# GpSimd prepares 48 weight chunks of the last mixer early and keeps their bf16 halves in DRAM; the last mixer's side work runs at four steps a chunk

## The chip, the cores and the metric

The kernel runs on one core of a Trainium2 chip. The metric is the device time in microseconds (us), the median of several runs. PE is TensorE, DVE is VectorE, ACT is ScalarE, POOL is GpSimd, SP is SyncE. L12 is line 12 of the kernel before.

## The reference

One sequence of 256 tokens, width 2048, goes through two blocks of two layers each. Cut to what matters:

```
first block (2 layers):
    short-conv mixer:  y = b * conv3(c * xv), then @ w_out
    conv FFN:          h = conv3(x @ w_up) + b;  (silu(g) * u) @ w_down
    shared k, v and differential attention;  conv FFN again
second block:
    ab_layer: dilated attention + gated linear attention, gate, @ w_out
    cd_layer (the last mixer):
        u, qd, fd, idd, gate = split(h @ cd_w_in)
        yc = s5_mixer(u)                 # complex diagonal state, scanned over time
        f  = lb + (1 - lb) * sigmoid(fd)
        od = chunked_gated_linear_attention(silu(qd), 1 - f, idd, log f)   # 8 heads ("hgrn")
        y  = concat(yc * sigmoid(yc @ w_glu + b), norm(od)) * silu(gate)
        h  = h + y @ cd_w_out
    final rmsnorm
```

All weights come as float32 and the products have to be near float32.

## The kernel before, in words

Activations lie transposed, features on partitions, 256 tokens along the free axis. Every large product is cut into weight chunks of 512 rows by 512 columns (1 MB of float32), 535 of them, in the fixed order of `weight_groups`. A group of chunks (four in most cases, two where an operand has 1024 rows) shares one PSUM tile; two PSUM tiles (PSG) alternate. A chunk goes through four engines:

- SP loads it into the ring WF of 3 slots (`load`, L410, the DMA at L415). It may do so once DVE is through with the chunk 3 before.
- ACT rounds it to bf16 into WH, a ring of 5 (`hi`, L994, the copy at L999), and adds one to `s_hi`. It waits for the load and for the matmuls of the chunk 5 before.
- DVE writes WL = WF - WH in bf16, again a ring of 5 (`lo`, L1485, the subtraction at L1489), and adds one to `s_lo`.
- PE waits for `s_lo` and issues 48 matmuls (`gemm`, L538, the matmul at L531): each 128x128 piece meets x as high x high, high x low, low x high. Then it adds one to `s_mm`.

ACT and DVE run `LA = 3` chunks ahead of PE, by the order in which their programs are written.

Everything that isn't a large product (attention, scans, norms) is a **side flow**, a Python generator on each engine. `side.step()` issues the next piece of the flow, and `gemm(..., rate=r)` decides how many pieces go beside one chunk: PE takes one after the second of the chunk's four row blocks and `max(1, r - 1)` behind the chunk; ACT and DVE take r. `side.until(flow)` issues all that is left of a flow at once. Every engine's order is fixed when the program is written.

In the last mixer the groups come in the order u (8 chunks), fd, qd, idd (8 each), three gate groups (12), glu (4), the last gate group (4), cd_out0 (8) and cd_out1 (8). Behind u two side flows start. `s5` has 16 iterations; in each PE multiplies the inputs (`product`), DVE does 10 instructions (L2070 to L2091, the scan at L2081 among them), and PE reads the result out into PSUM; after each second iteration DVE adds that (L2097). POOL's queue loads a rotation table for each iteration and output weights for each second one, ACT fills the scan's decay. `hgrn` has 8 heads: POOL subtracts the decays (`decays`, L438, lines 449 to 452), ACT exponentiates (L1291), DVE weights them (L1904), PE makes two sets of 8 products, DVE masks and sums each (L1914, L1918), PE multiplies with v and takes the norm. With rate 3, `hgrn` ends in front of cd_out1.

POOL is idle from 1.2 us on until the second FFN of the first block at 1487 us. The scratch SCR has a free stretch at `TR` until the attention of the first block (the stages before it are the first mixer, its output, and the first FFN: 196 chunks).

```
nc.vector.wait_ge(s_hi, i + 1)
tt(l, w, h, ALU.subtract).then_inc(s_lo, 1)          # lo(i), DVE
nc.tensor.wait_ge(s_lo, i + 1)                       # gemm, PE
if kk == 1 and rate > 1:
    side.step()
last.then_inc(s_mm, 1)
for _ in range(max(1, rate - 1)):
    side.step()
```

Of the kernel before, what the change touches and what calls it, by code (L numbers as in the profile page):

```python
# [195 lines left out]
def two_block_model(nc, A, out):  # L196
    ctx = ExitStack()
    with ctx:
# [10 lines left out]
        WH = sb("WH", [128, RB, 4, 512], BF16)  # L209
        WL = sb("WL", [128, RB, 4, 512], BF16)  # L210
# [17 lines left out]
        d_w = [sem(f"d_w{i}") for i in range(RF)]  # L228
        d_out = [sem(f"d_out{i}") for i in range(2)]
# [37 lines left out]
        groups, stage, chunks = weight_groups(A)  # L267

# [92 lines left out]
        T1, T2, T3 = (scr(TR + 3840 + 512 * n, 2, T) for n in range(3))  # L361
        CSD = nc.dram_tensor("s5_rotation", (16, 128, 4 * T), F32).ap()
# [46 lines left out]
        def sync_program():  # L409
            def load(i):  # L410
                g, k0, rows = chunks[i]
                src = g["w"][k0:k0 + rows, g["col"]:g["col"] + g["width"]].rearrange("(t p) n -> p t n", p=128)
                if i >= RF:
                    nc.sync.wait_ge(s_lo, i - RF + 1)
                nc.sync.dma_start(shaped(WF, i % RF, rows, g["width"]), src).then_inc(d_w[i % RF], 16)  # L415
# [9 lines left out]
            for i in range(RF, len(chunks)):  # L425
# [9 lines left out]
        def gpsimd_program():  # L435
# [21 lines left out]
            nc.gpsimd.memset(CX[:, :, 0:2], 0.0).then_inc(s_ones, 1)  # L457

# [67 lines left out]
        def tensor_program():  # L526
# [11 lines left out]
            def gemm(gi, xh, xl, ready=None, row_major=False, rate=1, before=None, tail=None):  # L538
# [6 lines left out]
                for c, k0 in enumerate(g["rows"]):  # L545
# [5 lines left out]
                    nc.tensor.wait_ge(s_lo, i + 1)  # L551
# [411 lines left out]
            for name in ("fd", "qd"):  # L963
                for gi in stage[name]:
                    gemm(gi, xh, xl, rate=3)
            for gi in stage["idd"]:
                gemm(gi, xh, xl, row_major=True, rate=3)
            flags.add("idd")
            for gi in stage["cd_gate"][0:3]:
                gemm(gi, xh, xl, rate=3)  # L970
            side.until(s5_flow)
            uh, ul = columns_of(UH), columns_of(UL)
            for n, gi in enumerate(stage["glu"]):
                gemm(gi, uh, ul, [(s_ul, k // 4 + 1) for k in range(8)] if n == 0 else None, rate=3)
            gated_0 = side.add_first(gated((0,)))
            gemm(stage["cd_gate"][3], xh, xl, rate=3)
            gated_1 = side.add_first(gated((1,)))
            gated_h = side.add(gated((2, 3)))
            residual("cd_out0", None, uh, ul, [(s_gl, 5 + k // 4) for k in range(8)], rate=3,
# [8 lines left out]
        def scalar_program():  # L988
# [446 lines left out]
            for j, gi in enumerate(stage["fd"]):  # L1435
                keep(gi, four(FF, j), 3, func=ACT.Sigmoid)
                nc.scalar.wait_ge(s_kd, j + 1)
                act(four(FF, j), four(FF, j), ACT.Ln).then_inc(s_fg, 1)
            for j, gi in enumerate(stage["qd"]):
                keep(gi, four(QH, j), 3, func=ACT.Silu)  # L1440
            for j, gi in enumerate(stage["idd"]):
                keep(gi, VI[:, :, 512 * j:512 * j + 512], 3, row_major=True)
# [21 lines left out]
            keep(gates[3], four(GT1, 1), 3, func=ACT.Silu)  # L1464
# [7 lines left out]
            residual("cd_out0", None, rate=3, before=lambda c: side.until(gated_0, *((gated_1,) if c else ())))  # L1472
# [6 lines left out]
        def vector_program():  # L1479
# [658 lines left out]
            for j, gi in enumerate(stage["fd"]):  # L2138
                gemm(gi, rate=3)
# [11 lines left out]
            for gi in stage["qd"] + stage["idd"]:  # L2151
                gemm(gi, rate=3)
            flags.add("idd")
            gates = stage["cd_gate"]
            for gi in gates[0:3]:
                gemm(gi, rate=3)
            side.until(s5_flow)
            for j, gi in enumerate(stage["glu"]):
                gemm(gi, rate=3)
# [14 lines left out]
            gemm(gates[3], rate=3)  # L2174
# [9 lines left out]
            residual("cd_out0", None, rate=3, before=lambda c: side.until(gated_0, *((gated_1,) if c else ())))  # L2184
# [70 lines left out]
```

## Time and profile before

| | |
|---|---|
| median of 3 runs | 3213.49 us (3213.07 to 3217.09) |
| the profiled execution: its own time | 3213.27 us |
| the profiled execution: span of the trace | 3212.0 us |
| PE busy | 3055.3 us, 95% |
| PE weight loads busy | 2600.1 us, 81% |
| DVE busy | 2129.2 us, 66% |
| ACT busy | 1527.7 us, 48% |
| POOL busy | 164.7 us, 5% |
| HBM read, written | 577.32 MB, 15.73 MB |

The matmuls are pipelined, so PE's busy time is not PE at its peak. A share of busy time is an average over stages with different limits; what the change touches are two stretches, the first 1084 us and the last 520 us, and they are to be read apart.

### The profile page before, as it was taken

What the parts mean: (1) busy time and instruction counts of PE and PEld (TensorE: products, weight loads), DVE (VectorE), ACT (ScalarE), POOL (GpSimd) and SP (SyncE); (2) the same over time, 40 slices, a digit from 0 to 9 for tenths busy, and PEclk for the clock granted to TensorE, in tenths of its full rate; (3) what the DMA queues carried; (4) which work ended last, traced back from release to release, by engine and by line L of the source; (5) the groups of instructions that cost most, each with busy time, mean ns of one, the idle gap of its engine ahead of it and who ended that gap; (6) DMA issues with size and microseconds to landing.
All of it is one profiled execution on the core that took longest, in us unless ns stands there. A gap on an engine that the chain in (4) does not pass through costs nothing. (4 is left out here: it accounts for less than half of the span.)

```text
span 3212.0 us, 57240 instructions
## 1 busy us (share of the span) xinstructions
PE 3055.3 (95%) x25845; PEld 2600.1 (81%) x25870; DVE 2129.2 (66%) x2024; ACT 1527.7 (48%) x1406; POOL 164.7 (5%) x292
## 2 busy tenths in 40 slices
PE   8999899999999999999999999998999899789896
PEld 7888788888888787587888888887686787657785
DVE  5555766666556666458687786555665547898785
ACT  4343654445434544745555555334554534333652
POOL 0000000000000000001200000000400000002220
PEclk9999999999999999999999999999999999899998
DMA  8665456655656454445766666563545445554331
GB/s 287 208 205 191 139 203 210 209 197 195 225 185 210 149 172 167 169 158 166 260 236 213 228 230 216 205 202 115 171 157 188 167 171 186 171 184 168 119 135 62
DMA packets 295477, 596.75 MB, mean 186 GB/s; under 512 B 11825, under 2 KB 16049, under 8 KB 295105
## 3 DMA queue, kind: packets, MB, share of 16 engines
q1 hardware_dynamic: 287616, 564.22, 51.4%
q0 software_dynamic: 7616, 28.87, 2.4%
q8 instruction: 203, 3.33, 0.4%
q14 instruction: 42, 0.34, 0.0%
HBM read 577.32 MB, written 15.73 MB: 185 GB/s over the span
## 5 line engine op out<-in xcount | busy, mean ns | idle before, releaser
L1489 DVE TENSOR_TENSOR WL<-WF,WH 128x2048 bf16<-128x2048 f32 x533 | 1208.5, 2288 | 682.3 <-ACT WH L999 682.1
L531 PE MATMUL PSG<-XH,WH 128*128 128x256 bf16 x5648 | 1549.9, 274 | 52.4 <-DVE XL L1594 26.3
L531 PE MATMUL PSG<-XL,WH 128*128 128x256 bf16 x5648 | 1549.7, 274 | 0.0
L531 PE MATMUL PSG<-XH,WL 128*128 128x256 bf16 x5648 | 1548.8, 274 | 0.0
L999 ACT ACTIVATE WH<-WF 128x2048 bf16<-128x2048 f32 x533 | 999.9, 1899 | 615.4 <-PE PSG L531 372.2
L531 PE MATMUL PSG<-SCR,WH 128*128 128x256 bf16 x4480 | 736.8, 273 | 0.0
L531 PEld LDWEIGHTS PSG<-XH,WH 128*128 128x128 bf16 x5648 | 556.4, 99 | 134.7 <-issue 65.5
L531 PEld LDWEIGHTS PSG<-XL,WH 128*128 128x128 bf16 x5648 | 555.9, 98 | 69.9 <-issue 1.2
L531 PEld LDWEIGHTS PSG<-XH,WL 128*128 128x128 bf16 x5648 | 556.1, 98 | 67.8
L531 PE MATMUL PSG<-SCR,WL 128*128 128x256 bf16 x2240 | 610.6, 273 | 0.0
L531 PEld LDWEIGHTS PSG<-SCR,WH 128*128 128x128 bf16 x4480 | 438.5, 98 | 55.0
L531 PEld LDWEIGHTS PSG<-SCR,WL 128*128 128x128 bf16 x2240 | 219.2, 98 | 25.5
L531 PE MATMUL PB<-SCR 128*128 128x128 f32 (+3 forms) x928 | 165.9, 347 | 53.0 <-DVE SCR L2091 32.2
L531 PEld LDWEIGHTS PB<-SCR 128*128 128x128 f32 (+2 forms) x928 | 137.1, 206 | 75.8 <-DVE SCR L2091 36.9
L1713 DVE SCALAR_TENSOR_TENSOR SCR<-PSG,PR,SCR 128x254 f32<-128x254 f32 (+1 forms) x352 | 143.9, 474 | 54.9 <-ACT SCR L1172 53.8
L1172 ACT ACTIVATE SCR<-PSG,PR 128x256 f32<-128x256 f32 x176 | 84.9, 562 | 102.6 <-PE PSG L531 102.4
L1020 ACT ACTIVATE SCR<-PSG 128x1024 f32<-128x1024 f32 x34 | 34.7, 1021 | 181.8 <-PE PSG L531 181.8
L531 PE MATMUL PSG<-WL,XH 128*128 128x512 bf16 x314 | 119.3, 380 | 1.0 <-issue 0.5
L531 PE MATMUL PSG<-WH,XL 128*128 128x512 bf16 x314 | 119.3, 380 | 0.3
L531 PE MATMUL PSG<-WH,XH 128*128 128x512 bf16 x307 | 116.8, 381 | 0.3
L461 POOL DMA_DIRECT2D SCR<-s_cT_re x1 | 0.7, 696 | 1486.2 <-DVE XL L1594 1486.2
L1183 ACT ACTIVATE SCR<-SCR 128x1024 bf16<-128x1024 f32 x22 | 23.2, 1057 | 96.1 <-DVE SCR L1722 96.1
(240 smaller groups left out, 1652.5 us busy)
## 6 DMA issues: line engine op xcount, KB each, us to landing
WF<-ffn_w_up SPq DMA_DIRECT2D x176, 1024.0 KB, 5.8
WF<-ffn_w_down SPq DMA_DIRECT2D x88, 1024.0 KB, 5.1
WF<-ab_w_in SPq DMA_DIRECT2D x56, 1024.0 KB, 5.2
WF<-a_w_in SPq DMA_DIRECT2D x48, 1024.0 KB, 6.0
WF<-cd_w_in SPq DMA_DIRECT2D x48, 1024.0 KB, 5.2
WF<-a_w_out SPq DMA_DIRECT2D x16, 1024.0 KB, 5.1
WF<-kv_w_k SPq DMA_DIRECT2D x16, 1024.0 KB, 5.1
WF<-b_w_q SPq DMA_DIRECT2D x16, 1024.0 KB, 5.1
```

Of the source, the lines that this page charges most:

```text
L461: nc.gpsimd.dma_start(CT[i].rearrange("p a b -> p (a b)"), A[name]).then_inc(d_s5c, 16)
L531: return nc.tensor.matmul(o, lhsT, rhs, start=start, stop=stop, skip_group_check=True)
L999: act(shaped(WH, i % RB, rows, g["width"]), shaped(WF, i % RF, rows, g["width"]), ACT.Copy).then_inc(s_hi, 1)
L1020: act(dst, rowwise(ps) if row_major else ps[:, :, :], func, scale=scale).then_inc(s_evac[gi % 2], 1)
L1172: t = act(dst[:, n, :], ps[:, n, :], ACT.Identity, bias=pr("f_bias", 88 * l + f), scale=pr("f_conv", 264 * l + 176 + f))
L1183: act(four(HH, j), HF, ACT.Copy).then_inc(s_hh, 1)
L1489: tt(l, w, h, ALU.subtract).then_inc(s_lo, 1)
L1713: ins = stt(dst[:, n, sh:T], ps[:, n, 0:T - sh], pr("f_conv", 264 * l + 88 * tap + f), dst[:, n, sh:T], ALU.mult, ALU.add)
```

## The change

The last mixer's first 48 chunks behind u (fd, qd, idd, all gates, glu and half of cd_out0) become **kept** chunks. From the sixth finished WL on, POOL takes them in 96 pieces of 256 rows: it loads a piece into scratch (512 KB), casts it to bf16, stores the high half (256 KB), subtracts, and stores the low half (256 KB), all into a DRAM tensor `weight_halves`. In the last mixer SP loads both halves of a kept chunk with one DMA of 1 MB straight into the ring of bf16 halves; ACT's cast and DVE's subtraction of these chunks are gone, and PE waits for the DMA. SP in front of the first kept load, and ACT in front of the first attention group, wait until all 96 pieces are stored. WH and WL become two views of one tensor WS. From fd on to cd_out0, rate 3 becomes rate 4.

```diff
-        WH = sb("WH", [128, RB, 4, 512], BF16)
-        WL = sb("WL", [128, RB, 4, 512], BF16)
+        WS = sb("WS", [128, RB, 2, 4, 512], BF16)
+        WH, WL = WS[:, :, 0, :, :], WS[:, :, 1, :, :]
...
+        first_kept = groups[stage["fd"][0]]["first"]
+        HALVES = nc.dram_tensor("weight_halves", (KEPT, 128, 2, 2048), BF16).ap()
...
+        KW = scr(TR, 2, 512)
+        KH, KL = scr(TR + 1024, 2, 512, dt=BF16), scr(TR + 1536, 2, 512, dt=BF16)
...
             def load(i):
+                if kept(i):
+                    nc.sync.wait_ge(s_mm, i - RB + 1)
+                    nc.sync.dma_start(WS[:, i % RB], HALVES[i - first_kept].rearrange("p h (t n) -> p h t n", n=512)
+                                      ).then_inc(d_ws[i % RB], 16)
+                    return
...
+            nc.sync.wait_ge(d_kh, 32 * KEPT)
+            nc.sync.wait_ge(d_kl, 32 * KEPT)
+            for i in range(first_kept, len(chunks)):
                 load(i)
...
+            def keep(n):
+
+                g, k0, rows = chunks[first_kept + n // 2]
+                a = 1024 * (n % 2)
+                src = g["w"][k0 + a // 4:k0 + a // 4 + 256, g["col"]:g["col"] + 512]
+                nc.gpsimd.dma_start(KW, src.rearrange("(t p) n -> p t n", p=128)).then_inc(d_keep, 16)
+                to_h, to_l = (HALVES[n // 2][:, i, a:a + 1024].rearrange("p (t n) -> p t n", n=512) for i in range(2))
+                nc.gpsimd.wait_ge(d_keep, 16 * (n + 1))
+                if n:
+                    nc.gpsimd.wait_ge(d_kh, 16 * n)
+                t = own.mark(nc.gpsimd.tensor_copy(KH, KW))
+                nc.gpsimd.wait_ge(g_own, t)
+                nc.gpsimd.dma_start(to_h, KH).then_inc(d_kh, 16)
+                if n:
+                    nc.gpsimd.wait_ge(d_kl, 16 * n)
+                t = own.mark(nc.gpsimd.tensor_tensor(KL, KW, KH, ALU.subtract))
+                nc.gpsimd.wait_ge(g_own, t)
+                nc.gpsimd.dma_start(to_l, KL).then_inc(d_kl, 16)
+
+            nc.gpsimd.wait_ge(s_lo, 6)
+            for n in range(2 * KEPT):
+                keep(n)
...
-                    nc.tensor.wait_ge(s_lo, i + 1)
+                    nc.tensor.wait_ge(*halves_there(i))
...
             def hi(i):
+                if kept(i):
+                    return
...
             pairs, outs = [], []
+            nc.scalar.wait_ge(d_kh, 32 * KEPT)
+            nc.scalar.wait_ge(d_kl, 32 * KEPT)
...
             def lo(i):
+                if kept(i):
+                    return
...
-                gemm(gi, rate=3)
+                gemm(gi, rate=4)
```

What it moves, at three places. The names are those of the program; SCR is the scratch, PB the PSUM banks of the side flows, PSG those of the large products.

POOL, start of the program. Before, a table load of the second FFN follows the memsets:

```order
L457 MEMSET SCR 128x4x2
L461 DMA SCR<-s_cT_re 128x512
L461 DMA SCR<-s_cT_im 128x512
L462 MEMSET SCR 128x1280
```

Now:

```order
L488 MEMSET SCR 128x4x2
L495 DMA SCR<-cd_w_in 128x2x512
L500 CAST SCR<-SCR 128x1024
L502 DMA weight_halves<-SCR 128x1024
L505 ISA
L505 TENSOR_TENSOR SCR<-SCR 128x1024
L507 DMA weight_halves<-SCR 128x1024
```

Five of these rows (without ISA) come 96 times in front of everything that POOL did before.

DVE, last mixer, one iteration of s5 in the middle of the gate groups, before:

```order
L2070 TENSOR_TENSOR SCR<-PB,SCR 128x1024
L2071 TENSOR_TENSOR SCR<-PB,SCR 128x1024
L2073 TENSOR_TENSOR SCR<-SCR 128x512
L2074 TENSOR_TENSOR SCR<-SCR 128x512
L1489 TENSOR_TENSOR WL<-WF,WH 128x2048
L2081 SCALAR_TENSOR_TENSOR SCR<-SCR 128x512 x2
L2086 TENSOR_TENSOR SCR<-SCR 128x1024
L2088 TENSOR_TENSOR SCR<-SCR 128x1024
L2090 TENSOR_TENSOR SCR<-SCR 128x512
L2091 TENSOR_TENSOR SCR<-SCR 128x512
L1489 TENSOR_TENSOR WL<-WF,WH 128x2048
L2097 SCALAR_TENSOR_TENSOR SCR<-SCR,PR,PB 128x256
```

Now:

```order
L2132 TENSOR_TENSOR SCR<-PB,SCR 128x1024
L2133 TENSOR_TENSOR SCR<-PB,SCR 128x1024
L2135 TENSOR_TENSOR SCR<-SCR 128x512
L2136 TENSOR_TENSOR SCR<-SCR 128x512
L2143 SCALAR_TENSOR_TENSOR SCR<-SCR 128x512 x2
L2148 TENSOR_TENSOR SCR<-SCR 128x1024
L2150 TENSOR_TENSOR SCR<-SCR 128x1024
L2152 TENSOR_TENSOR SCR<-SCR 128x512
L2153 TENSOR_TENSOR SCR<-SCR 128x512
L2159 SCALAR_TENSOR_TENSOR SCR<-SCR,PR,PB 128x256
```

The subtractions between and behind the iteration are gone, so L2153 and L2159 are neighbours.

PE, last mixer, the last head of hgrn, before (it stands in front of cd_out1, nothing of a large product between the groups):

```order
L531 MATMUL PB<-SCR 128x256
L531 MATMUL PB<-SCR 128x128 x10
L531 MATMUL PB<-SCR,ONE_128 128x256
L531 MATMUL PB<-SCR 128x128 x8
L531 MATMUL PB<-SCR 128x256
L531 MATMUL PB<-SCR 128x128
L531 MATMUL PB<-SCR,ONE_128 128x256
```

Now, a head of hgrn beside glu:

```order
L585 MATMUL PB<-SCR 128x128 x9
L585 MATMUL PB<-SCR,ONE_128 128x256
L585 MATMUL PB<-SCR 128x128 x8
L585 MATMUL PSG0<-SCR,WS 128x256 x48
L585 MATMUL PB<-SCR 128x256
L585 MATMUL PB<-SCR 128x128
L585 MATMUL PSG0<-SCR,WS 128x256 x48
L585 MATMUL PB<-SCR 128x128 x9
L585 MATMUL PB<-SCR,ONE_128 128x256
L585 MATMUL PB<-SCR 128x128 x8
```

A head takes two chunks, all eight heads end in the last gate group, and the two sets of products (x9 and x8) now have no chunk between them.

## Rows read from the trace of the kernel before

**Rows 1.** Stretches of the program: busy time of each engine, clock, DMA share.

```profile
core 0: us, PE busy (x) PEld busy (x) DVE busy (x) ACT busy (x) POOL busy (x), PEclk, DMA share, GB/s
372.00:833.00 461.00, 459.75 (x4213) 411.86 (x4211) 301.42 (x301) 235.01 (x210) 0.00 (x0) 1.00 0.58 201
2696.00:2952.00 256.00, 216.84 (x1482) 160.63 (x1486) 231.96 (x209) 90.42 (x95) 18.20 (x35) 0.94 0.53 174
2952.00:3146.00 194.00, 168.44 (x1397) 150.42 (x1395) 154.59 (x206) 114.75 (x120) 60.71 (x119) 0.92 0.36 124
3146.00:3213.00 67.00, 49.75 (x398) 41.74 (x398) 32.33 (x32) 16.26 (x12) 0.00 (x0) 0.86 0.18 64
```

**Rows 2.** Waits of PE, 2696 to 2952 us: waited for, us in total, times, longest.

```profile
PE PB L531 <- DVE SCR L2091: 32.2, 13, 8.6
```

**Rows 3.** Groups of instructions, 2696 to 2952 us: DVE's subtractions.

```profile
L1489 DVE TENSOR_TENSOR WL<-WF,WH 128x2048 bf16<-128x2048 f32 x30 | 68.5, 2284 | 10.6 <-ACT WH L999 10.5
```

**Rows 4.** Timeline of DVE in s5: start us, us, instruction.

```profile
2701.36 1.22 DVE L2070 TENSOR_TENSOR SCR<-PB,SCR 128x1024 f32<-128x1024 f32 x1
...
2836.20 1.22 DVE L2070 TENSOR_TENSOR SCR<-PB,SCR 128x1024 f32<-128x1024 f32 x1
...
2845.47 0.69 DVE L2091 TENSOR_TENSOR SCR<-SCR 128x512 f32<-128x512 f32 x1
...
2951.31 0.48 DVE L2097 SCALAR_TENSOR_TENSOR SCR<-SCR,PR,PB 128x256 f32<-128x256 f32 x1 [1.68 <-PE PB L531]
```

**Rows 5.** The chain that ended last, near its end: one chunk on PE.

```profile
3187.63 5.25 PE PSG L531 x48
```

**Rows 6.** Timeline of PE: the groups of an s5 iteration and of a head.

```profile
2831.67 1.89 PE L531 MATMUL PB<-SCR 128*128 128x256 f32 x8
2850.77 1.13 PE L531 MATMUL PB<-SCR 32*128 32x256 f32 x8
...
3105.68 0.82 PE L531 MATMUL PB<-SCR 128*128 128x256 f32 x4
3111.57 2.23 PE L531 MATMUL PB<-SCR 128*128 128x128 f32 x18
3114.26 0.67 PE L531 MATMUL PB<-SCR,ONE 128*128 128x256 f32 x2 [0.46 <-ACT SCR L1299]
3117.39 1.95 PE L531 MATMUL PB<-SCR 128*128 128x128 f32 x16
```

**Rows 7.** Start and end of POOL's room: timelines of DVE and of ACT.

```profile
33.07 2.29 DVE L1489 TENSOR_TENSOR WL<-WF,WH 128x2048 bf16<-128x2048 f32 x1 [0.31 <-ACT WH L999]
...
1082.87 5.50 ACT L999 ACTIVATE WH<-WF 128x2048 bf16<-128x2048 f32 x3
```

**Rows 8.** DMA issues: 1590 to 1965 us, then 2696 to 2952 us: KB each, us to landing.

```profile
s_rotation<-SCR POOLq DMA_DIRECT2D x16, 512.0 KB, 6.1
...
SCR<-s_rotation POOLq DMA_DIRECT2D x14, 512.0 KB, 3.5
```

**Rows 9.** Groups of instructions of POOL, shapes kept apart.

```profile
L477 POOL DMA_DIRECT2D s_rotation<-SCR x16 | 8.5, 533 | 360.6 <-ACT SCR L1272 360.6
...
L484 POOL MEMSET SCR<- 128x1024 f32 x1 | 1.0, 952 | 9.7 <-DVE XL L1594 9.7
```

**Rows 10.** Timeline of POOL, at 1591 us and in the ab mixer.

```profile
1591.81 0.53 POOL L474 DMA_DIRECT2D s_outputs<-SCR  x1 [0.30 <-POOL SCR L471]
...
2270.30 2.44 POOL L450 TENSOR_TENSOR SCR<-SCR 128x128 f32<-128x128 f32 x1
...
2275.11 0.40 POOL L450 TENSOR_TENSOR SCR<-SCR 128x128 f32<-128x128 f32 x1
```

**Rows 11.** Timeline of DVE, beside POOL's decays.

```profile
2267.79 7.10 DVE L1489 TENSOR_TENSOR WL<-WF,WH 128x2048 bf16<-128x2048 f32 x3
...
2955.80 2.60 DVE L1489 TENSOR_TENSOR WL<-WF,WH 128x2048 bf16<-128x2048 f32 x1 [4.01 <-ACT WH L999]
```

More of the change, by code:

```diff
@@ L27 @@
 LA = 3
+KEPT = 48
 MAGIC = 12582912.0
@@ L228, in two_block_model @@
         d_w = [sem(f"d_w{i}") for i in range(RF)]
+        d_ws = [sem(f"d_ws{i}") for i in range(RB)]
+        d_keep, d_kh, d_kl = sem("d_keep"), sem("d_kh"), sem("d_kl")
         d_out = [sem(f"d_out{i}") for i in range(2)]
@@ L424, in sync_program @@
             nc.sync.dma_start(POSI, A["positions"].partition_broadcast(128)).then_inc(d_pos, 16)
-            for i in range(RF, len(chunks)):
+            for i in range(RF, first_kept):
+                load(i)
+            nc.sync.wait_ge(d_kh, 32 * KEPT)
+            nc.sync.wait_ge(d_kl, 32 * KEPT)
+            for i in range(first_kept, len(chunks)):
                 load(i)
@@ L973, in tensor_program @@
             for n, gi in enumerate(stage["glu"]):
-                gemm(gi, uh, ul, [(s_ul, k // 4 + 1) for k in range(8)] if n == 0 else None, rate=3)
+                gemm(gi, uh, ul, [(s_ul, k // 4 + 1) for k in range(8)] if n == 0 else None, rate=4)
             gated_0 = side.add_first(gated((0,)))
-            gemm(stage["cd_gate"][3], xh, xl, rate=3)
+            gemm(stage["cd_gate"][3], xh, xl, rate=4)
             gated_1 = side.add_first(gated((1,)))
             gated_h = side.add(gated((2, 3)))
-            residual("cd_out0", None, uh, ul, [(s_gl, 5 + k // 4) for k in range(8)], rate=3,
+            residual("cd_out0", None, uh, ul, [(s_gl, 5 + k // 4) for k in range(8)], rate=4,
                      before=lambda c: side.until(gated_0, *((gated_1,) if c else ())))
@@ L1435, in scalar_program @@
             for j, gi in enumerate(stage["fd"]):
-                keep(gi, four(FF, j), 3, func=ACT.Sigmoid)
+                keep(gi, four(FF, j), 4, func=ACT.Sigmoid)
                 nc.scalar.wait_ge(s_kd, j + 1)
@@ L1439, in scalar_program @@
             for j, gi in enumerate(stage["qd"]):
-                keep(gi, four(QH, j), 3, func=ACT.Silu)
+                keep(gi, four(QH, j), 4, func=ACT.Silu)
             for j, gi in enumerate(stage["idd"]):
-                keep(gi, VI[:, :, 512 * j:512 * j + 512], 3, row_major=True)
+                keep(gi, VI[:, :, 512 * j:512 * j + 512], 4, row_major=True)
             flags.add("idd")
@@ L1446, in scalar_program @@
             for j, gi in zip(GATE_ORDER[0:3], gates[0:3]):
-                keep(gi, four(GT1, j), 3, func=ACT.Silu)
+                keep(gi, four(GT1, j), 4, func=ACT.Silu)
             side.until(s5_flow)
             for j, gi in enumerate(stage["glu"]):
-                ps = gemm(gi, rate=3)
+                ps = gemm(gi, rate=4)
                 nc.scalar.wait_ge(s_mm, done(gi))
@@ L1463, in scalar_program @@
             gated_0 = side.add_first(gated_s5(0))
-            keep(gates[3], four(GT1, 1), 3, func=ACT.Silu)
+            keep(gates[3], four(GT1, 1), 4, func=ACT.Silu)
             gated_1 = side.add_first(gated_s5(1))
@@ L1471, in scalar_program @@
             gated_h = side.add(gated_hgrn())
-            residual("cd_out0", None, rate=3, before=lambda c: side.until(gated_0, *((gated_1,) if c else ())))
+            residual("cd_out0", None, rate=4, before=lambda c: side.until(gated_0, *((gated_1,) if c else ())))
             side.until(gated_h)
@@ L1485, in lo @@
             def lo(i):
+                if kept(i):
+                    return
                 g, _, rows = chunks[i]
-                w, h, l = (shaped(t, i % n, rows, g["width"]) for t, n in ((WF, RF), (WH, RB), (WL, RB)))
-                nc.vector.wait_ge(s_hi, i + 1)
+                r = raw(i)
+                w, h, l = (shaped(t, n, rows, g["width"]) for t, n in ((WF, r % RF), (WH, i % RB), (WL, i % RB)))
+                nc.vector.wait_ge(s_hi, r + 1)
                 tt(l, w, h, ALU.subtract).then_inc(s_lo, 1)
@@ L2155, in vector_program @@
             for gi in gates[0:3]:
[L2156 removed]
+                gemm(gi, rate=4)
             side.until(s5_flow)
             for j, gi in enumerate(stage["glu"]):
[L2159 removed]
+                gemm(gi, rate=4)
                 for n in range(0, 4, 2):
@@ L2183, in vector_program @@
             gated_h = side.add(gated_hgrn())
-            residual("cd_out0", None, rate=3, before=lambda c: side.until(gated_0, *((gated_1,) if c else ())))
+            residual("cd_out0", None, rate=4, before=lambda c: side.until(gated_0, *((gated_1,) if c else ())))
             side.until(gated_h)
```

29 lines of the change are left out of this document (19 added, 10 removed).

## Prediction, on record before the run

> **What bounds the kernel now.** I read the stretches first, then the waits of PE and the timeline of DVE where PE has holes, and last the rows that price POOL's new work. In the first FFN PE is busy 459.75 of 461 us at clock 1.00, DVE 301 us [rows 1]: PE is the bound, and 160 us of DVE are free. In the last mixer it is otherwise. While s5 runs, DVE is busy 231.96 of 256 us and PE 216.84, at clock 0.94 [rows 1]; PE waits 32.2 us for the last instruction of an iteration, L2091 [rows 2]. s5 takes from 2701.36 to 2951.79, 250.4 us for 16 iterations [rows 4], and 30 subtractions of 2284 ns lie among them [rows 3]. So DVE is the bound of this stretch. While hgrn runs, to 3146 us, neither is full (PE 168, DVE 155 of 194 us) and the clock is 0.92 [rows 1]: there the turns between engines cost. The clock falls to the 1.2 GHz level only where PE had holes.
>
> **The sum, last mixer.** A chunk costs PE 5.25 us [rows 5]. Behind u there are 60 chunks: 8 of them run after 3146 us as before, 52 up to there.
>
> *s5 on DVE.* An iteration without subtractions is 2836.20 to 2846.16, 9.96 us less the overlap of neighbours, 9.9 us [rows 4]; 16 make 158 us. Eight L2097 of 0.4 us make 3; the two fd groups and the scan of the hgrn decays, some 10 us, stay. That is 171 us. Before, the subtractions covered DVE's wait for PE's output products; now L2097 stands right behind its iteration and waits for a group of 1.89 us plus a hand-over [rows 6], 2.2 us eight times, 18 us. DVE also waits for PE at the two fd groups, 4 us each by my estimate. Sum 197 us instead of 250. PE in that time: an iteration has 5.5 steps, some 93 in all, thus 23 chunks at four steps (31 at three). 23 x 5.25 = 121 us plus 16 x (1.89 + 1.13) = 48 us [rows 6] is 169 us, so PE waits 28 us and DVE stays the bound. What PE doesn't do here it does later.
>
> *From there to 3146.* 29 chunks (52 - 23) are 152 us, the eight heads 8 x (2.23 + 0.67 + 1.95 + 0.82) = 45 us [rows 6]. Waits: 3 us until the first head's weights are there, 3 behind the last, and per head 1.5 us, since the second set of products now follows the first directly and needs DVE's masking of it. A head takes two chunks, 5.7 us of its own and the wait, some 17.7 us; the turn over POOL's decays and ACT's exponentials may be as long, which the bound of 19 us holds. Sum 152 + 45 + 18 = 215 us instead of 194. Together 412 instead of 445 us: **33 us gained**. Bounds: 50 where L2097's wait and the heads' waits vanish, 10 where an iteration needs 13 us and a head 19.
>
> ACT's 48 casts go too; ACT was busy 90 of 256 us [rows 1], so that gives nothing. The kept load waits for the ring's slot and has four chunks, 21 us, to land: nothing.
>
> **The sum, first 1084 us.** POOL may start when the sixth subtraction ends, 33.07 + 2.29 = 35.4 us. ACT meets its new wait behind the layer norm, at 1082.9 us [rows 7]. Behind it are queued all casts of the attention stage, and behind these DVE's subtractions and PE, which has three chunks in hand. SP's new wait comes 1600 us later and costs nothing. The room is 1047.5 us for 96 pieces, **10.9 us a piece**. A piece is a chain, since the scratch is single:
>
> - load of 512 KB, issue to landing: 3.5 us with little beside it, 6.1 us (a store) in an FFN where weights stream [rows 8]. The engines move data 0.58 of the time [rows 1]. I take the middle, 4.8.
> - cast of 1024 columns: a memset of that size takes 0.952 us [rows 9]. Taken 0.95; 1.3 at most.
> - subtraction: a two-input operation on 128 columns takes 0.40 us [rows 10], eight times that is 3.2; below, two passes like the memset, 1.9. I take 2.4, since the small one has a start in it that the large one pays once.
> - twice hand-over and DMA issue, 0.30 + 0.53 [rows 9, 10]: 1.66.
> - GpSimd's small operation took 2.44 us instead of 0.40 while DVE ran three subtractions back to back [rows 10, 11]: it waited for the whole of one. Two such operations per piece, DVE in a subtraction 2.2 of 5.25 us, half of that left: 0.5 each, 1.0.
>
> Sum 10.8 us; 96 pieces end at 35.4 + 1038 = 1073 us, 10 us in front of the wait. The ends: 7.9 us (load 3.5, subtraction 1.9, no blocking: done at 790) and 13.5 us (load 6.1, cast 1.3, subtraction 3.2, blocking 1.2: done at 1331). Both the kind of price and the place of the deadline are close, so lateness is the main rival.
>
> The Trainium skill's GPSIMD Engine Reference, section 3.1, gives 4497 ns for a two-input float32 operation of 2048 columns. Half of it is an estimate of 2.25 us for the subtraction; by it a piece would take 10.65 us and the last one would end at 1058.
>
> What it costs the others: POOL's two operations hold DVE off. DVE has 160 us of 461 to spare, and 3.4 us of POOL in 10.8 delay a subtraction by some 0.3 us on average; PE has three chunks ahead. The added 96 MB come to some 90 GB/s beside 201 and lengthen the weight loads by one or two us, and a slot of the ring of three has 15.75 us for load, cast and subtraction, which take 10. I take **4 us** lost, 0 to 15.
>
> 3213.3 (the profiled execution; the median is 0.2 above) - 33 + 4 = 3184 us.
>
> **Rivals.**
>
> *Late pieces (slower).* The place is ACT's wait in front of kq, the price what POOL still has to do. From 10.9 us a piece on, PE starves. Then weights no longer stream and DVE is still, and a piece takes 3.5 + 0.95 + 2.4 + 1.66 = 8.5 us. At 12 us a piece 87 are done by 1083, nine are left, 77 us: 3184 + 77 - 3 = 3258. The gain is used up at 11.3 us a piece (29 us late), and it is slower by over 0.2% from 11.4 on. For it: the stores of rows 8 needed 6.1 us in such a stage, and a load stands behind the low half's store in POOL's queue. Against it: those stores were issued just when a weight load was, and around the two layer norms little streams. Chance 0.27, and 0.10 for a little late, 3190 to 3215.
>
> *DVE and POOL block each other (slower).* A subtraction beside POOL's decays took 2.60 us instead of 2.28 [rows 11, 3]. If DVE, ACT and the loads came so late in the FFN that the ring of three fills only as fast as PE eats, each of 88 FFN chunks would lose 0.7 us, 62 us over the 88 and less elsewhere; at half of that, 3184 + 31 + 5 = 3220. Against it: DVE's 160 free us. Chance 0.06. The Trainium skill's page SBUF — State Buffer, section on the two separate sides, says that the pair of ports which the two engines share is an exclusive lock for a whole instruction, against a VectorE operation with two SBUF inputs. By that rule, the trace agrees for POOL's side (2.44 instead of 0.40), and hardly for DVE's side.
>
> *The last mixer is bound by its turns.* DVE waits for PE and PE for DVE in every iteration, 13 us each; the gain is 10 us, 3207 us. For it: 13 waits of up to 8.6 us [rows 2]. Chance 0.07.
>
> That the change doesn't do what it says I rule out by the order of the instructions: 30 subtractions have left the s5 stretch and the heads end in front of cd_out0.
>
> **How the numbers follow.** In time, 3184 us: 0.50. A measurement of this kernel tells a difference from 0.2%, 6.4 us. Faster: 0.50, 0.06 of the slightly late, 0.03 of the turns, 0.59. Same: 0.03 + 0.04 = 0.07. Slower: 0.27 + 0.06 + 0.01 = 0.34. The range: down to 3165 (a gain of 48 us; 0.05 lies below), up to 3275, where a piece needs 12.3 us; the upper end of my price, 13.5 us, would give some 3340 and is left out with 0.08. The likeliest case alone spans 3165 to 3200.
>
> **What would show it.** POOL's stores end before 1083 us, and no wait of ACT for a store of weight_halves is in the list; pieces of 10 to 11 us; DVE's busy time down by 48 x 2.28 = 109 us; s5 from first to last in 190 to 205 us; a head in 17 to 19 us; the last 16 chunks without side work. Wrong is the prediction if PE has one hole of tens of us near 1090 us (the first rival), if the first FFN takes over 465 us (the second), or if an s5 iteration takes 13 us (the third).

## The result, and the profile after

| | before | after |
|---|---|---|
| median | 3215.29 us (4 runs) | 3252.06 us (4 runs, 3249.79 to 3271.64) |
| profiled execution, its own time | 3213.27 us | 3271.64 us |
| span of the trace | 3212.0 us | 3270.3 us |

The ratio is 1.013 with a 95% interval of 1.0112 to 1.0148: the change makes the kernel slower. The medians are 36.8 us apart and the two profiled executions 58.4, since the profiled one of the change was the slowest of its four. Where its 58 us come from is read in three places. The stretches first (line numbers are now those of the changed kernel):

```profile
core 0: us, PE busy (x) PEld busy (x) DVE busy (x) ACT busy (x) POOL busy (x), PEclk, DMA share, GB/s
461.00:922.00 461.00, 461.00 (x4223) 412.83 (x4222) 331.74 (x263) 220.75 (x184) 224.16 (x190) 1.00 0.84 291
1090.00:1190.00 100.00, 17.51 (x140) 14.43 (x138) 17.81 (x11) 14.17 (x17) 49.07 (x49) 0.60 0.33 104
2800.80:2993.20 192.40, 168.96 (x1139) 123.99 (x1140) 166.65 (x179) 31.43 (x58) 17.86 (x34) 0.96 0.52 188
2993.20:3204.30 211.10, 199.28 (x1679) 172.59 (x1678) 121.79 (x193) 95.56 (x111) 48.19 (x120) 0.98 0.41 148
```

In the first FFN of this execution PE is as full as in [rows 1], though the DMA engines are busy 0.84 of the time instead of 0.58 and POOL half of it. But between 1090 and 1190 us PE works 17.5 of 100 us. The waits of that place, of ACT and of PE:

```profile
ACT WS L1056 <- DMA weight_halves<-SCR: 80.7, 1, 80.7
```

```profile
PE PSG L585 <- DVE WS L1551: 79.9, 1, 79.9
```

ACT waits 80.7 us for the last store of a half, DVE's subtraction stands behind ACT's cast, and PE behind that. It is one wait, in front of the attention stage. In [rows 7] ACT's casts of that stage begin at 1082.87; now:

```profile
1101.16 1.06 ACT L1148 ACTIVATE XH<-XA 128x1024 bf16<-128x1024 f32 x1
1182.90 5.51 ACT L1056 ACTIVATE WS<-WF 128x2048 bf16<-128x2048 f32 x3 [80.69 <-DMA weight_halves<-SCR]
```

ACT is ready at 1102.2, so 19.3 us are lost already before the wait. That is the second place. The delay was 3 us at the 64th finished low half, 16 us at the 80th and 16 at the 192nd: it comes about around the layer norm in front of the first FFN, and the last 4 us come in the layer norm in front of the attention. The timelines of DVE and of POOL in the first of the two:

```profile
359.43 2.12 DVE L1666 TENSOR_TENSOR XA<-XA,STAT 128x256 f32<-128x256 f32 x1 [1.71 <-ACT STAT L1136]
...
367.90 2.83 DVE L1656 TENSOR_TENSOR XL<-XA,XH 128x256 bf16<-128x256 f32 x1
...
378.03 3.15 DVE L1666 TENSOR_TENSOR XA<-XA,STAT 128x1024 f32<-128x1024 f32 x1
```

```profile
359.12 2.13 POOL L505 TENSOR_TENSOR SCR<-SCR 128x1024 bf16<-128x1024 f32 x1
...
368.31 2.14 POOL L505 TENSOR_TENSOR SCR<-SCR 128x1024 bf16<-128x1024 f32 x1
...
377.90 2.20 POOL L505 TENSOR_TENSOR SCR<-SCR 128x1024 bf16<-128x1024 f32 x1
```

Each long DVE instruction lies on one of POOL's subtractions. Before, the same instructions (L1604 and L1594 there) took 0.42 us (256 columns) and 1.22 us (1024 columns):

```profile
356.42 0.42 DVE L1604 TENSOR_TENSOR XA<-XA,STAT 128x256 f32<-128x256 f32 x1 [1.71 <-ACT STAT L1079]
...
362.47 0.42 DVE L1594 TENSOR_TENSOR XL<-XA,XH 128x256 bf16<-128x256 f32 x1
...
369.66 1.22 DVE L1604 TENSOR_TENSOR XA<-XA,STAT 128x1024 f32<-128x1024 f32 x1
```

PE has no chunk in hand in a layer norm, and its waits are of this kind (340 to 460 us):

```profile
PE PSG L585 <- DVE XL L1656: 9.7, 4, 6.9
PE PB L585 <- DVE SCR L1801: 4.0, 1, 4.0
```

Before, the same two were 5.8 and 1.2 us.

The third place is the last mixer. The first instruction of s5 on DVE and the last L2159:

```profile
2800.84 1.23 DVE L2132 TENSOR_TENSOR SCR<-PB,SCR 128x1024 f32<-128x1024 f32 x1 [15.40 <-PE PB L585]
```

```profile
2992.78 0.48 DVE L2159 SCALAR_TENSOR_TENSOR SCR<-SCR,PR,PB 128x256 f32<-128x256 f32 x1 [3.67 <-PE PB L585]
```

s5 takes 192.4 us instead of 250.4 [rows 4]. From its first instruction to the end of the span it is 469.5 us instead of 510.6 (3212.0 - 2701.36). The account closes: s5 begins 99.5 us late (2800.84 - 2701.36), 80.7 of it the wait and some 19 from the early stages (80.7 and 19.3 make 100.0, of which 0.5 is made good until s5); 41.1 us are won after that; 58.4 us remain, and the spans differ by 58.3.

What a piece costs is in POOL's groups (the first four, of which L495 stands here with its `cd_w_in` loads alone) and in a timeline, at 711 us beside the FFN and at 1142 us, where PE, ACT and DVE stand still:

```profile
L505 POOL TENSOR_TENSOR SCR<-SCR 128x1024 bf16<-128x1024 f32 x96 | 248.6, 2590 | 1.6
L500 POOL CAST SCR<-SCR 128x1024 bf16<-128x1024 f32 x96 | 139.9, 1458 | 515.2 <-DMA SCR<-cd_w_in 435.1 <-DMA SCR<-s_w_glu 48.1 <-DMA SCR<-cd_w_out 32.0
L495 POOL DMA_DIRECT2D SCR<-cd_w_in x80 | 58.0, 725 | 36.4 <-DVE WS L1551 34.4 <-issue 2.0
L502 POOL DMA_DIRECT2D weight_halves<-SCR x96 | 53.6, 558 | 30.7 <-POOL SCR L500 28.3 <-issue 2.4
```

```profile
711.99 0.72 POOL L495 DMA_DIRECT2D SCR<-cd_w_in  x1
718.77 1.03 POOL L500 CAST SCR<-SCR 128x1024 bf16<-128x1024 f32 x1 [6.06 <-DMA SCR<-cd_w_in]
720.10 0.56 POOL L502 DMA_DIRECT2D weight_halves<-SCR  x1 [0.30 <-POOL SCR L500]
720.67 2.14 POOL L505 TENSOR_TENSOR SCR<-SCR 128x1024 bf16<-128x1024 f32 x1
723.11 0.56 POOL L507 DMA_DIRECT2D weight_halves<-SCR  x1 [0.30 <-POOL SCR L505]
...
1142.02 0.72 POOL L495 DMA_DIRECT2D SCR<-cd_w_out  x1
1146.94 1.03 POOL L500 CAST SCR<-SCR 128x1024 bf16<-128x1024 f32 x1 [4.19 <-DMA SCR<-cd_w_out]
```

The load's time from issue to landing, over the whole kernel (DMA issues: count, KB each, median us):

```profile
SCR<-cd_w_in POOLq DMA_DIRECT2D x80, 512.0 KB, 6.2
```

On average of 96: issue 0.72, wait for the load 5.37 (515.2 / 96), cast 1.46, subtraction 2.59, two store issues 1.12, two hand-overs 0.6. That is 11.9 us, and the distance between loads is 11.96. In the still stretch a piece took 9.7 us. When ACT was ready, at 1102.2, the load of the 89th piece was just about to go out (1103.83): 88 were done, eight were left, 78 us and the landing of the last store.

### The profile page after: what moved, and what is told of

It is laid out like the page before. It is cut to its first block and busy times, and to the rows that moved or that the text cites. A ratio compares the mean times of both kernels' runs of the same rounds, so it can differ in the third digit from the quotient of the medians.

```text
span 3270.3 us, 57700 instructions
## 1 busy us (share of the span) xinstructions
PE 3052.8 (93%) x25870; PEld 2592.5 (79%) x25870; DVE 2126.4 (65%) x1976; ACT 1443.8 (44%) x1360; POOL 716.1 (22%) x772
## 5 line engine op out<-in xcount | busy, mean ns | idle before, releaser
L585 PE MATMUL PSG<-XH,WS 128*128 128x256 bf16 x11296 | 1893.4, 275 | 132.7 <-DVE WS L1551 97.0
L1551 DVE TENSOR_TENSOR WS<-WF,WS 128x2048 bf16<-128x2048 f32 (+1 forms) x485 | 1179.2, 2454 | 696.8 <-ACT WS L1056 696.5
L585 PE MATMUL PSG<-XL,WS 128*128 128x256 bf16 x5648 | 1552.4, 275 | 0.0
L585 PEld LDWEIGHTS PSG<-XH,WS 128*128 128x128 bf16 x11296 | 1113.4, 99 | 285.3 <-DVE WS L1551 82.4
L1056 ACT ACTIVATE WS<-WF 128x2048 bf16<-128x2048 f32 (+1 forms) x485 | 909.6, 1899 | 698.8 <-PE PSG L585 298.0
L585 PE MATMUL PSG<-SCR,WS 128*128 128x256 bf16 x6720 | 743.1, 273 | 0.0
L585 PEld LDWEIGHTS PSG<-SCR,WS 128*128 128x128 bf16 x6720 | 658.0, 98 | 81.4
L585 PEld LDWEIGHTS PSG<-XL,WS 128*128 128x128 bf16 x5648 | 556.3, 98 | 70.2 <-issue 0.3
L500 POOL CAST SCR<-SCR 128x1024 bf16<-128x1024 f32 x96 | 139.9, 1458 | 515.2 <-DMA SCR<-cd_w_in 435.1
L505 POOL TENSOR_TENSOR SCR<-SCR 128x1024 bf16<-128x1024 f32 x96 | 248.6, 2590 | 1.6
L585 PE MATMUL PSG<-WS,XH 128*128 128x512 bf16 x640 | 191.2, 380 | 0.0
L585 PE MATMUL PB<-SCR 128*128 128x128 f32 (+3 forms) x928 | 155.7, 331 | 34.5 <-DVE SCR L2153 18.5
L1077 ACT ACTIVATE SCR<-PSG 128x1024 f32<-128x1024 f32 x34 | 34.7, 1020 | 175.6 <-PE PSG L585 175.5
```

Of the source, the lines that this page charges most:

```text
L500: t = own.mark(nc.gpsimd.tensor_copy(KH, KW))
L505: t = own.mark(nc.gpsimd.tensor_tensor(KL, KW, KH, ALU.subtract))
L585: return nc.tensor.matmul(o, lhsT, rhs, start=start, stop=stop, skip_group_check=True)
L1056: act(shaped(WH, i % RB, rows, g["width"]), shaped(WF, r % RF, rows, g["width"]), ACT.Copy).then_inc(s_hi, 1)
L1077: act(dst, rowwise(ps) if row_major else ps[:, :, :], func, scale=scale).then_inc(s_evac[gi % 2], 1)
```

## The experiments

Every profile was taken apart at the same point: when s5's first DVE instruction starts (before: 2701.36), and how long it is from there to the end of the span (before: 510.6 us).

| run | median | ratio to before, 95% | s5 starts later by | from there to the end |
|---|---|---|---|---|
| the change | 3252.06 | 1.013 (1.0112 to 1.0148) | 99.5 | 469.5 |
| e1 40 kept, rate 4 | 3201.22 | 0.9959 (0.9943 to 0.9975) | 16.1 | 483.0 |
| e2 early work of 40 alone | 3230.12 | 1.0041 (1.0026 to 1.0056) | 20.5 | 508.1 |
| e3 rate 4 alone | 3260.26 | 1.0133 (1.0117 to 1.0148) | -0.1 | 551.4 |
| e4 40 kept, rate 3 | 3179.58 | 0.9878 (0.9862 to 0.9895) | 21.6 | 461.7 |
| e5 POOL's computation alone | 3221.03 | 1.0024 (1.0015 to 1.0034) | 10.4 | 508.0 |
| e6 transfers alone | 3221.91 | 1.0023 (1.0011 to 1.0034) | 6.5 | 509.8 |
| e7 48, two buffers, rate 4 | 3204.61 | 0.9969 (0.9956 to 0.9982) | 26.9 | 469.5 |
| e8 48, two buffers, paced, rate 4 | 3182.18 | 0.9899 (0.9884 to 0.9913) | 7.2 | 469.5 |
| e9 as e8, rate 3 | 3157.53 | 0.9825 (0.9812 to 0.9838) | 6.4 | 446.3 |
| e10 as e9, with a pause | 3151.46 | 0.9802 (0.9789 to 0.9815) | 4.1 | 444.2 |
| e11 the change again | 3261.19 | 1.0143 (1.0113 to 1.0173) | 71.5 | 469.5 |
| e12 the change, rate 3 | 3237.69 | 1.0062 (1.004 to 1.0085) | 70.9 | 444.2 |

**e1_kept40.** Are the pieces late, or do POOL and its transfers slow the 196 chunks themselves?

```diff
-KEPT = 48
+KEPT = 40
```

> The change with 40 kept chunks instead of 48 (80 pieces; the last gate group and the first half of cd_out0 go the old way). Theory A, the pieces are late: in the profile of the change a piece took 12.0 us, ACT's wait lasted 80.7 us and the last mixer gave 41 us back. 80 pieces of 12.3 us end at 35.6 + 984 = 1020 us, 60 us in front of the wait, which vanishes. The layer norm in front of the first FFN still loses some 14 us: 3213 + 14 - 40 = 3187 us, 3170 if those 14 us were a chance of one execution. Theory B, POOL and the added transfers slow the first 196 chunks themselves: 80 of 96 parts of that loss stay and the time is over 3240 us.

Measured: 3201.2 us, and no wait for a store in ACT's list. The 80 us of the wait are gone with the last 16 pieces, so theory A holds. It is still 14 us over the 3187 expected: the early part cost about what was expected (16 us for 14), but from s5 on it is 483.0 us and not 470. The eight chunks that lost their halves cost 13.5 us there. What they met shows in e3.

**e2_early40.** POOL does its 80 pieces, both waits stay, and the last mixer is as before (cut; the lines are against the change).

```diff
-KEPT = 48
+KEPT = 40
             def kept(i):
-                return first_kept <= i < first_kept + KEPT
+                return False
...
-                gemm(gi, rate=4)
+                gemm(gi, rate=3)
```

> POOL does the 80 early pieces, with both waits, but nobody uses the halves: the last mixer loads, casts and subtracts its chunks as before, at three side steps a chunk. This measures the price of the early work without a stall. Theory A: only the stretch around the layer norm in front of the first FFN is longer, 10 to 19 us, 3223 to 3232 us. Theory B: 3290 us or more. A third possibility, that the 14 us were a chance of that one execution: 3213 to 3218 us.

Measured: 3230.1 us, 13 us over before, as theory A said; the last mixer takes 508 us like before. Early work of 40 chunks costs 13 us without any stall. I had put down 4.

**e3_rate4_alone.** No kept chunks and no early work, only the rates (cut; the lines are against the kernel before).

```diff
-                gemm(gi, rate=3)
+                gemm(gi, rate=4)
```

> No kept chunks and no early work, only four side steps a chunk from fd on to cd_out0. If the gain in the last mixer comes from the subtractions that DVE no longer does, this gives nothing: DVE stays the bound of s5 with 30 subtractions less the denser side work, 3205 to 3220 us. If the gain comes from the rate, it gives most of the 41 us: 3175 to 3185 us.

Measured: 3260.3 us, 43 us slower than before, and all of it is in the last mixer (551 us instead of 511). Neither expectation saw that. PE's waits from 2701 us on, then DVE's timeline beside a head:

```profile
PE PB L580 <- issue: 35.2, 7, 7.3
PE PB L580 <- DVE SCR L2146: 34.7, 12, 5.7
PE PB L580 <- DVE SCR L2126: 16.8, 8, 8.0
```

```profile
3014.48 1.93 DVE L1973 TENSOR_REDUCE SCR<-SCR 128x128 f32<-128x1024 f32 x1
3021.40 2.59 DVE L1544 TENSOR_TENSOR WS<-WF,WS 128x2048 bf16<-128x2048 f32 x1 [4.99 <-ACT WS L1051]
3023.91 1.21 DVE L1969 TENSOR_TENSOR SCR<-PB,CN 128x1024 f32<-128x1024 f32 x1
```

PE's second set of products was done at 3016.6. Their masking, L1969, stands in DVE's order behind a subtraction, the subtraction waits for ACT's cast, and ACT is late since its own step of the head waited for PE. So the mask comes at 3023.9 and PE's next step of the head after that. As I read this head, with four steps a chunk the turns of a head and the path of the weights (ACT, DVE, PE) are locked into each other, seven waits of 5 us (35.2 in all; before, one of 3.3). The other two lines are s5's and add 13 us more (34.7 + 16.8 against 32.2 + 6.4). Kept chunks have no part on ACT and DVE, so they open this lock; in e1 PE's wait of this kind comes back twice, 13.7 us together and 7.3 at most, where its chunks are no longer kept.

**e4_kept40_rate3.** The halves without the higher rate.

```diff
-KEPT = 48
+KEPT = 40
...
-                gemm(gi, rate=4)
+                gemm(gi, rate=3)
```

> 40 kept chunks at three side steps a chunk. If DVE's freedom is the whole gain, this is as fast as 40 chunks at rate 4. If both are needed, s5 is now bound by PE: 31 chunks of 5.25 us and 48 us of its own, some 211 us instead of 192, and the heads again end in front of cd_out1 with PE waiting for their turns; 3195 to 3205 us where 40 chunks at rate 4 give 3187.

Measured: 3179.6 us, 1.2% under the kernel before where e1 was 0.4% under it, and 22 us faster than e1. The guess that both are needed was wrong in its sign: the higher rate costs 21 us (461.7 against 483.0). s5 took 208.5 us, as worked out, but with PE busy nearly all of it.

**e5_compute_only and e6_transfers_only.** What of the early 13 us is POOL's computation, what the transfers? e5 casts and subtracts scratch of zeros, e6 loads and stores with neither cast nor subtraction; both pace their 80 pieces by finished low halves, and in both the last mixer is as before. The diff is that of e5, against the change; e6 drops the cast and the subtraction instead of the transfers.

```diff
+                nc.gpsimd.wait_ge(s_lo, 6 + 7 * n // 3)
-                nc.gpsimd.dma_start(KW, src.rearrange("(t p) n -> p t n", p=128)).then_inc(d_keep, 16)
...
                 t = own.mark(nc.gpsimd.tensor_copy(KH, KW))
                 nc.gpsimd.wait_ge(g_own, t)
-                nc.gpsimd.dma_start(to_h, KH).then_inc(d_kh, 16)
...
                 t = own.mark(nc.gpsimd.tensor_tensor(KL, KW, KH, ALU.subtract))
                 nc.gpsimd.wait_ge(g_own, t)
-                nc.gpsimd.dma_start(to_l, KL).then_inc(d_kl, 16)
```

> POOL does the 80 casts and the 80 subtractions on scratch of zeros, one pair after every 2.33 finished low halves (12.2 us), without the loads and the stores; the last mixer is as before, so the halves are neither made nor used. The complete early work of 40 chunks cost 13 us against before (3230.1 against 3216.9). Theory 'port': the cost is DVE held off by POOL in the layer norm in front of the first FFN, where L1666 took 3.15 us instead of 1.22; then these 13 us stay, 3226 to 3232 us. Theory 'transfers': the cost is the denser DMA traffic, and this run gives 3215 to 3219 us.

> POOL's queue does the 80 loads and 160 stores at the same pace, with neither cast nor subtraction (the stored halves are zeros and nobody reads them); the last mixer is as before. Theory 'port': 3215 to 3219 us. Theory 'transfers': 3226 to 3232 us. If both share it, each of the two runs shows a part and the parts add up to about 13 us.

Measured: 3221.0 and 3221.9 us, 6.6 and 7.5 over before, so by the medians each is a part. The profiles say more. In e5 the 64th low half is 1.6 us late and the 80th 7.6 us, with PE waiting 3.8 us for L1788 there (before: 1.2): the place around the layer norm. In e6 the 80th and the 196th low half are at most 1.0 us late, so in this execution the transfers cost the first 196 chunks next to nothing; its loss is one wait behind them:

```profile
1091.39 5.51 ACT L1052 ACTIVATE WS<-WF 128x2048 bf16<-128x2048 f32 x3 [7.57 <-DMA weight_halves<-SCR]
```

That is my pacing: the 80th piece began too late. So e6 says that transfers by themselves, at this pace, don't slow this part, and its time is no measure of them. That e5 (8 us) and the full work (13 us) differ is open; in e5 the pace kept POOL out of the layer norm itself.

**e7_two_buffers and e8_two_buffers_paced.** The load of the next piece goes out ahead of the cast of this one; e8 adds a pace (the line with `wait_ge`, which e7 has not).

```diff
+            fetch(0)
             for n in range(2 * KEPT):
+                if n + 1 < 2 * KEPT:
+                    nc.gpsimd.wait_ge(s_lo, 6 + 15 * (n + 1) // 8)
+                    fetch(n + 1)
                 keep(n)
```

> The change with 48 chunks and rate 4, but two load buffers in scratch, so that the load of the next piece goes out ahead of the cast of this one. Nothing holds POOL back. If the wait for the load (5.4 of 12.2 us a piece) made the pieces late, a piece now takes 6.5 to 9 us, the last store lands before 900 us, and ACT waits for none: 3213 + 15 - 41 = 3187 us. If the transfers themselves are the limit (DMA share 0.84 already), a piece stays above 10.9 us or the weight loads come late and PE waits in the first stages: over 3215 us.

> As the run before, but the load of piece n waits for the low half 6 + 15 n / 8, so one piece goes out every 9.8 us and the last at the 184th of 196 chunks. Transfers are spread evenly. No stall in front of the attention; 3187 us by the same sum. If two buffers without a pace crowd out the weight loads, this run is faster than that one; if not, both are equal.

Measured: 3204.6 and 3182.2 us. Both have all 48 chunks, neither has a wait of ACT for a store, and both have the 469.5 us of the change from s5 on, to the tenth. So the single buffer, in which a load waits for the piece before, was the cause of the late pieces: in e7 a piece took 8.6 us. They differ in the early stages, 26.9 against 7.2 us. One stretch, 345 to 460 us, of e7 and then of e8:

```profile
345.00:460.00 115.00, 91.63 (x736) 76.73 (x734) 101.18 (x75) 53.64 (x62) 88.00 (x76) 0.90 0.78 264
```

```profile
345.00:460.00 115.00, 102.89 (x878) 89.30 (x877) 86.72 (x81) 63.13 (x70) 55.38 (x49) 0.94 0.72 254
```

Without a pace POOL is busy 88 of 115 us in the one stretch where PE has nothing in hand, and DVE needs 101 us for less work. From 460 to 750 us, where PE has its three chunks, even e7 holds PE at 289 of 290 us with the DMA engines at 0.91.

**e9_paced_rate3 and e10_paced_rate3_pause.** e9 is e8 with rate 3. e10 loads no piece between the 60th and the 72nd low half and one every 1.75 chunks outside of it (the lines are against e9).

```diff
+            def pace(n):
+                i = 6 + 7 * n // 4
+                return i if i < 60 else i + 12
...
-                    nc.gpsimd.wait_ge(s_lo, 6 + 15 * (n + 1) // 8)
+                    nc.gpsimd.wait_ge(s_lo, pace(n + 1))
```

> 48 kept chunks, two load buffers, loads paced by finished low halves, three side steps a chunk as before the change. In the profiles the stretch from the first instruction of s5 to the end took 466.5 us with rate 4 and 458.7 with rate 3 (40 kept chunks); if this holds for 48, it is 8 us faster than e8_two_buffers_paced: 3174 us. If the eight further kept chunks (last gate group, half of cd_out0), which run beside the heads, need the higher rate to be worth anything, it is 3182 us as before.

> As the run before, but no piece is loaded between the 60th and the 72nd finished low half, so that POOL is still around the layer norm in front of the first FFN; outside of it a piece goes out every 1.75 chunks. The price of the early work in e8_two_buffers_paced was 8 us, nearly all of it in that place. If it is the shared port, the pause gives back 5 to 8 us, 3167 to 3169 us; if it is the transfers of the denser rest, nothing, 3174.

Measured: 3157.5 and 3151.5 us. Rate 3 gave 24.7 us and not 8. The 8 was worked out from 466.5 and 458.7 us, which are not the lengths in the traces: for 40 chunks these are 483.0 and 461.7, a step of 21.3 us, and for 48 it is 23.2 (469.5 against 446.3). The eight further kept chunks are worth 15.4 us at this rate and 13.5 at rate 4. s5 and its surroundings in e9:

```profile
2707.00:2916.00 209.00, 200.27 (x1458) 152.09 (x1461) 166.67 (x179) 33.51 (x61) 18.10 (x35) 0.98 0.58 210
```

s5 is 16 us longer than in the change (208.1 against 192.4), but with some eight chunks more in it, 42 us of PE. PE, not DVE, bounds it now, busy 0.96 of the time instead of 0.88. The pause gave 6.1 us more. In e10 the stretch from 345 to 385 us is what it was before (e10 first, then before), and DVE's first instruction of the attention comes at 1099.7 us (before: 1100.0):

```profile
345.00:385.00 40.00, 34.01 (x276) 28.80 (x274) 31.18 (x36) 23.87 (x34) 0.00 (x0) 0.91 0.35 118
```

```profile
345.00:385.00 40.00, 34.20 (x276) 28.85 (x274) 31.19 (x36) 24.09 (x34) 0.00 (x0) 0.91 0.34 118
```

Its s5 starts 4.1 us late all the same; these come up behind the attention's start, and their cause is open.

From the first instruction of s5 to the end, before and then e10:

```profile
2701.36:3212.00 510.64, 429.67 (x3229) 348.42 (x3232) 416.68 (x446) 216.41 (x221) 78.91 (x153) 0.92 0.42 141
```

```profile
2705.47:3149.70 444.23, 406.81 (x3240) 336.22 (x3244) 318.23 (x401) 137.78 (x177) 69.77 (x153) 0.97 0.46 164
```

Of the 66.4 us between them 43.5 are idle time of PE (80.97 against 37.42). The other 22.9 are busy time for the same products, and the mean granted clock was 0.97 instead of 0.92; in e3, where PE had more holes than before, it was 0.91, and the same products took 439.6 us. So a third of the gain goes with the clock, which stood in none of my sums.

e10 is the version to keep: 2% faster than the kernel before (0.9802, 0.9789 to 0.9815), and 3% faster than the change.

**e11_change_again.** Why were the four runs 20 us apart?

> The change itself once more. Its profiled execution took 3271.6 us and the three others 3250 to 3253. If the length of the stall in front of the attention varies from execution to execution, the profile of this one shows a wait of ACT of another length than 80.7 us, and its time follows it one to one, after the 14 to 19 us of the early stages and minus 41 us in the last mixer: a wait of 60 us belongs to 3251 us.

Measured: six runs from 3243.6 to 3279.0 us. The profiled one took 3243.6, and its wait is

```profile
ACT WS L1056 <- DMA weight_halves<-SCR: 45.5, 1, 45.5
```

s5 starts 71.5 us late instead of 99.5, and from there on it is the same 469.5 us: all of the difference lies in front. The wait does not follow one to one as I expected, since ACT was ready later here (1109.8 instead of 1102.2): 26.9 us lost early and 45.5 of wait are 72.4, of which 0.9 is made good until s5. Its 96 pieces took 11.66 us each instead of 11.96, which over 96 is 28.5 us. A serial chain of 96 pieces turns 0.3 us a piece into 28 us of the kernel.

Why ACT was ready later matters too. The 80th low half is 16 us late as in the change, but the 196th 23 us, where in the change it stayed at 16: PE lost time in the streaming FFN. The stretch, and PE's wait in it:

```profile
461.00:922.00 461.00, 455.90 (x4155) 406.75 (x4154) 321.76 (x262) 217.70 (x183) 225.67 (x203) 1.00 0.84 292
```

```profile
PE PSG L585 <- DVE WS L1551: 5.1, 5, 2.7
```

That wait was 8.3 us in e12's profiled execution and 3.7 in e4's, and e2 had none. What decides it is open.

**e12_change_rate3.** The change with its single buffer, at rate 3.

> The change with its 48 chunks and its single load buffer, but three side steps a chunk. With two paced buffers the step from rate 4 to rate 3 gave 25 us (3182.2 to 3157.5), in a part of the program that the late pieces do not touch. If the two causes add up, this run is 23 to 25 us faster than the change, 3227 to 3236 us, and still slower than before, because ACT's wait of 50 to 80 us stays. If the rate were the whole loss of the change, it would be under 3214 us.

Measured: 3237.7 us, 23.5 us under e11 and still slower than before. From s5 on it is 444.2 us, as in e10; the wait of ACT was 38.5 us in the profiled execution, the shortest of seven (3217.8 to 3246.8). In front of s5 it lost what e11 lost (70.9 and 71.5 us), and behind it is 25.3 us shorter, so the two causes add up.

## Why the prediction was wrong

**The step that failed is the price of a piece, 10.8 us.** Everything hung on it, since the room was 10.9. Term by term, predicted and measured (mean of 96): load 4.8 and 6.1 (0.72 issue, 5.37 wait); cast 0.95 and 1.03 where it stood alone; subtraction 2.4 and 2.13 alone; hand-overs and store issues 1.66 and 1.72; blocking 1.0 and 0.89 (1458 - 1030 and 2590 - 2130 ns). Four of the five terms are right to 0.3 us. The load is wrong by 1.3 us: I took "the middle" between 3.5 us in a quiet stretch and 6.1 us in a streaming FFN [rows 8], although the pieces run in such a stage. The load's kind also differs from the quiet row: with the other engines still, it took 4.7 us on average (0.72 and a wait of 4.0) and not 3.5. The argument "around the two layer norms little streams" bore on a few of the 96 pieces. With 6.1 for the load my own sum gives 12.1 us, and the pieces are late. (Its low end adds up to 8.0 us and not 7.9; nothing hangs on that.)

**The late-pieces rival is what came.** It said: at 12 us a piece 87 are done, nine are left, 77 us, 3258 us. Measured: 11.96 us, 88 done, eight left, 80.7 us, and 3252 us as the median. That 3258 is so near is in part luck: the early stages lost 19 us and not 4, a piece in the still stretch took 9.7 us and not 8.5, the mixer gave 41 us and not 33, and the profiled execution itself took 3271.6. Its point of decision, 11.4 us, is borne out as far as 11.66 and 11.96 lie above it; no run came nearer. e1 and e8 take the cause away in two ways, and the wait goes. What was mis-weighed was its chance, 0.27: a serial chain of 96 with 1% of room, whose own bounds ran from 7.9 to 13.5 us, is no better than even, and the row nearest to its conditions stood at the slow end.

**The early cost was put at 4 us, in truth 13 (e2) to 27 (e11) with the single buffer.** Where PE has three chunks ahead the reasoning was near: DVE's low halves took 2698 ns on average up to 1083 us (before, 2289 ns) and the DMA share was 0.84, and PE lost nothing in the change and in e2, 3.7 to 8.3 us in e4, e11 and e12. It left out the place where nothing is ahead, the layer norm and the first chunks of the FFN. "3.4 us of POOL in 10.8 delay a subtraction by 0.3 us on average" was an average where single instructions of 0.42 us waited 2 us in a chain. e10 shows the place: POOL quiet there, and the loss is gone. I also took the blocking on DVE's side as hardly borne out, from a 2.60 us row beside small decays; beside 1024 columns it is plain (3.15 us instead of 1.22). The Trainium skill's page SBUF — State Buffer, section on the two separate sides, says that the loser is held for the whole instruction; by that rule, the trace agrees on this side too.

**The last mixer was right in size and wrong in its reason.** Predicted 33 us, measured 41; s5 197 and 192.4 us; a head 17 to 19 us, measured 16.4 (from L1980 at 3020.2 to the same one of the next head at 3036.6); PE's waits in s5 28 us, measured 23.5 (18.5 for L2153 and 5.0 for L2133). But I booked rate 4 as part of the gain. It is a loss: 40.8 us without kept chunks (e3), 21 us with 40 and 23 with 48. Kept halves alone give 64 us (510.6 to 446.3), and about a third of that is the granted clock, which the sum left out. PE busy 0.88 of s5 was to be read as PE not full, in a kernel that PE bounds: what the side work won by ending early, PE lost by waiting for it.

The rival of DVE and POOL blocking each other named a real mechanism and put its weight in the wrong place: of its 62 us in 88 FFN chunks, PE lost none in the row 461 to 922 us of the change and 5.1 in that of e11. The rival of the turns, 13 us an s5 iteration, did not come: an iteration took 192.4 / 16 = 12.0 us.

## What to carry to other kernels

Work that one engine does ahead of time in a serial chain, behind a fixed deadline, is to be priced at the row that was measured in the stage where it will run, and its room has to bear the scatter times the number of links; two buffers and a pace tied to the main loop's counter took one more stretch of scratch and made 3252 us into 3182. Work in the free time of a helper engine was cheap where the bound engine had work in hand (0 to 8 us here), and dear where it had none: keep the helper still around norms and stage starts. When a change moves two knobs, measure each alone; here the rate, which looked like the harvest of the kept halves, was a loss of 23 us hidden under a gain of 64.

## What was not expected of the hardware

- A DVE instruction of 256 columns took 2.12 and 2.83 us instead of 0.42 where one of POOL's of 1024 columns ran, and POOL's cast took 1.46 us on average instead of 1.03, its subtraction 2.59 instead of 2.13.
- A DMA of 512 KB from POOL's queue in rows of 2 KB took 0.72 us to issue, and with the other engines still POOL went on 4.0 us later on average (3.4 to 4.5); over all 96 it was 6.1 us in all. Its issue is longer than the 0.53 us of the rotation's DMA of the same size [rows 9].
- PE held 461.00 of 461 us busy with the DMA engines at 0.84 in the change, and 289 of 290 us at 0.91 in e7; but in two more executions of the same early work, also at 0.84, it was 455.90 (e11) and 452.66 (e12).
- With fewer holes in PE the granted clock rose from 0.92 to 0.97 from s5 on, and PE's products there took 406.81 us of busy time instead of 429.67.
- Executions of one program agreed within 0.3% in the kernel before; those of the change lie 35 us apart (3243.6 to 3279.0). In the two that have a profile the chain of 96 pieces ends 28 us apart, and so does the kernel.
